# Unread products of old operands on TensorE inside its waits, in a two-layer hybrid trunk

## The reference, cut to what matters

```python
h = rmsnorm(x, norm1_g) * (1 + sc1) + sh1          # first norm
... = project_in(h, w_in)                          # then four token mixers
gate = sigmoid(h @ w_gate + b_gate)
merged = einsum('blnd,blnd->bld', gate, proj)      # proj: mixers @ w_branch
x = x + g1 * (merged @ w_out)
h2 = rmsnorm(x, norm2_g) * (1 + sc2) + sh2         # second norm
x = x + g2 * hier_moe(h2, ...)                     # 16 experts, top-1 group, top-2 expert
```

## Time and profile before

| | us |
|---|---|
| median of 3 runs | 2670.8 |
| lowest and highest | 2663.51, 2673.95 |
| the profiled execution's own time | 2673.33 |
| its span, first to last instruction | 2671.5 |
| mean granted TensorE clock in it | 0.942 |

### The profile page before, as it was taken

One profiled execution on the slowest core, in us unless ns is written; L12 is line 12 of the kernel. 1 busy time (PEld: TensorE's weight loads), 2 busy tenths in 40 slices (PEclk: granted clock), 3 DMA queues, 4 the chain that ended last, 5 costly groups with the idle time before them and its releaser, 6 DMA issues. The chain is left out here.

```text
span 2671.5 us, 33821 instructions
## 1 busy us (share of the span) xinstructions
PE 2484.2 (93%) x11748; PEld 1961.7 (73%) x11749; DVE 2061.3 (77%) x2682; ACT 1275.4 (48%) x1774; POOL 8.2 (0%) x16
## 2 busy tenths in 40 slices
PE   5699978999999998999998998799999999899997
PEld 2388745888888874878776886588888887777876
DVE  1499434888888874699898984488888888579988
ACT  2244243344343431688776443443434343277876
POOL 0000000000000000000000000000000000000000
PEclk8899887999999997899998998799999999799998
DMA  8988755776767658499886876277676675279986
GB/s 357 371 307 287 283 210 220 270 255 226 258 222 261 238 197 315 163 344 364 326 315 230 294 241 254 108 292 254 234 247 241 236 252 189 98 258 338 372 297 232
DMA packets 116660, 698.36 MB, mean 261 GB/s; under 512 B 24876, under 2 KB 30924, under 8 KB 33712
## 3 DMA queue, kind: packets, MB, share of 16 engines
q1 hardware_dynamic: 116528, 696.54, 71.4%
HBM read 691.97 MB, written 4.52 MB: 261 GB/s over the span
## 5 line engine op out<-in xcount | busy, mean ns | idle before, releaser
L607 ACT ACTIVATE high_w<-raw_w 128x1024 fp32r<-128x1024 f32 x904 | 942.9, 1054 | 794.2 <-PE bank L1633 684.1
L980 DVE TENSOR_TENSOR low_w<-raw_w,high_w 128x1024 fp32r<-128x1024 f32 x904 | 1076.7, 1211 | 180.4 <-ACT high_w L607 174.1
L1631 PE MATMUL bank<-high_w,in_high 128*128 128x512 f32 (+1 forms) x1600 | 625.0, 391 | 16.3 <-DVE low_w L980 16.3
L1632 PE MATMUL bank<-low_w,in_high 128*128 128x512 f32 (+1 forms) x1600 | 620.5, 388 | 0.0
L1633 PE MATMUL bank<-high_w,in_low 128*128 128x512 f32 (+1 forms) x1600 | 620.5, 388 | 0.0
L1631 PEld LDWEIGHTS bank<-high_w,in_high 128*128 128x128 f32 x1600 | 303.2, 190 | 89.3 <-issue 29.5
L1000 DVE SCALAR_TENSOR_TENSOR gate_mod_acc<-gate_mod_w,cond,gate_mod_acc 128x512 f32<-128x512 f32 x480 | 339.5, 749 | 23.3 <-issue 2.3
L1633 PEld LDWEIGHTS bank<-high_w,in_low 128*128 128x128 f32 x1600 | 302.9, 189 | 60.8
L1632 PEld LDWEIGHTS bank<-low_w,in_high 128*128 128x128 f32 x1600 | 303.2, 190 | 59.6
L2027 PE MATMUL bank<-high_w,win_high 128*128 128x512 f32 x512 | 206.2, 403 | 12.0 <-issue 6.7
L2028 PE MATMUL bank<-low_w,win_high 128*128 128x512 f32 x512 | 202.2, 395 | 0.0
(11 more groups left out here) (236 smaller groups left out, 2630.5 us busy)
## 6 DMA issues: line engine op xcount, KB each, us to landing
raw_w<-in_w_gate SPq DMA_DIRECT2D x128, 1024.0 KB, 5.0
raw_w<-in_w_exp_gate_up SPq DMA_DIRECT2D x128, 1024.0 KB, 5.5
mod_w<-in_w_mod SPq DMA_DIRECT2D x96, 1024.0 KB, 7.9
raw_w<-in_w_in SPq DMA_DIRECT2D x64, 1024.0 KB, 5.7
gate_mod_w<-in_w_mod SPq DMA_DIRECT2D x64, 1024.0 KB, 7.1
raw_w<-in_w_exp_down SPq DMA_DIRECT2D x64, 1024.0 KB, 5.3
in_mod_w<-in_w_mod SPq DMA_DIRECT2D x32, 1024.0 KB, 7.1
raw_w<-in_w_branch SPq DMA_DIRECT2D x32, 1024.0 KB, 5.0
```

Source lines behind the costliest of these rows:

```text
L607: act.activation(high_w[:, part, ks, 0:width], raw_w[:, slot, ks, 0:width], ACT.Copy).then_inc(high_ready, 1)
L980: dve.tensor_tensor(low_w[:, part, ks, 0:width], raw_w[:, slot, ks, 0:width], high_w[:, part, ks, 0:width].bitcast(F32), ALU.subtract).the ...
L1631: pe.matmul(out, highs[:, kk, t, :], high_w[:, part, k, 0:width], start=start, stop=False)
L1632: pe.matmul(out, highs[:, kk, t, :], low_w[:, part, k, 0:width], start=False, stop=False)
```

## The change

A helper keep_clock makes a number of 128x512 products of an operand with itself (its first 128 columns stand still, its 512 columns move) into one bank. Nothing reads the results, and the next use of the bank starts afresh. It is called in four places of TensorE's program:

- at the start of layer 1, in front of its first norm: 20 products of hid_low, after a new wait until three of layer 0's four additions are done;
- in front of the wait for the last merged values, in both layers: 12 products of in_high;
- in front of the second norm, in both layers: 24 products of in_high;
- in front of the last return, in both layers: 9 products of hid_high, into the bank of the chunk pair that has been read.

The operands are those of products that are over.

```diff
--- before.py
+++ after.py
@@ -1681,6 +1681,11 @@
             def turn(bank, col, src, width=P):
                 return pe.transpose(bank[:, col:col + width], src, ident[0:src.shape[0], 0:src.shape[0]])
 
+            def keep_clock(bank, operand, products):
+
+                for _ in range(products):
+                    pe.matmul(bank[:, :], operand[:, 0:P], operand, start=True, stop=True)
+
             def route_logits(i):
 
                 t, g = i // KB, i % KB
@@ -1736,6 +1741,8 @@
 
             for l in range(DEPTH):
                 if l:
+                    pe.wait_ge(added, NCH * l - 1)
+                    keep_clock(turn_banks[0], hid_low[:, 0:2, :, :].rearrange("p k t n -> p (k t n)"), 20)
                     turn_quarter(l, 0)
 
                 def before_unit(j):
@@ -1914,12 +1921,14 @@
                         if b == 3:
                             dense_sums(mod_bank, gate_mod_acc, (1,), used)
                 at.rounds(pe, NCH, gates, {n: k for n, k in W_OUT_SLOTS.items() if n[:2] != "in"} | {"chunk": NCH, "merged": TILES})
+                keep_clock(turn_banks[0], in_high[:, 0:2, :, :].rearrange("p k t n -> p (k t n)"), 12)
                 pe.wait_ge(chunk_read, at.done("chunk"))
                 turn_merged()
                 w_out()
                 pe.wait_ge(dense_stored, STORES * (l + 1))
 
                 pe.wait_ge(router_in, 32 * (l + 1))
+                keep_clock(turn_banks[0], in_high[:, 0:2, :, :].rearrange("p k t n -> p (k t n)"), 24)
                 norm2(len(mod_stage(l, "norm")) * UPC // (2 * KB))
                 mod_step(0)
 
@@ -2098,6 +2107,7 @@
                             if g or h or not at.first:
                                 back(back_banks[h if g else (h + 1) % 2], (g - 1) % GROUP_N, at.done("chunk") - 1)
                 at.rounds(pe, NCH // 2, down_pair)
+                keep_clock(banks[2 * (at.done("chunk") % 2)], hid_high[:, 0:2, :, :].rearrange("p k t n -> p (k t n)"), 9)
                 back(back_banks[1], GROUP_N - 1, at.done("chunk"))
 
         @block.gpsimd
```

## The result

The changed kernel took 2653.04 us in the median of 6 runs (2647.81 to 2659.5), the kernel before 2668.18 us on the same chip (6 runs, 2660.01 to 2673.95). The ratio is 0.9949, with a 95% interval of 0.9926 to 0.9973: faster, by 15 us. The forecast was 2663.5 us with a range of 2656 to 2671, so the time lies outside, on the fast side, and "faster by over 0.5%", which the median just is (0.51%) and the interval leaves open, had been given 0.13. Against the kernel before, 7.3 us less was forecast (2663.5 beside the 2670.8 of its first three runs), and 15.1 us less was measured (2653.04 beside the 2668.18 of six). Three more comparisons of the two kernels came later: ratios 0.9937 [0.9918, 0.9955], 0.9956 [0.9941, 0.9972] and 0.9936 [0.9917, 0.9955].

What follows compares the result with a forecast made beforehand. TensorE, busy 93% of the span, was taken as the bound, with half clock behind waits. Gains 3.3 + 3.2 + 1.8 + 0.5 + 0.5 = 9.3 us took 2673.33 to 2664.0; median put at 2663.5, range 2656 to 2671.

Steps and rivals of the forecast that it cites:

- The step that failed: TensorE's whole program: fetching the 220 added instructions was costed at nothing, beside weight transfers that run anyway.
- Merge: Last merged values and w_out: products and transposes at full instead of half clock, gaining 3.3 us in layer 0, 3.2 in layer 1.
- Rival 1: The clock falls after the block at the merge; each merge keeps 0.5 us, time 2668.5 us; chance 0.22.
- Last returns: Last return in each layer: four products at full clock and an earlier end, 0.9 us each, 1.8 together.
- the first norm: Layer 1's start: the first four transposes run at full clock, 0.45 us faster, counted as a gain of 0.5 us.
- Second norm, layer 1: First transposes start fast, gaining 0.5 us; the clock was expected to fall early in the loop.
- Second norm, layer 0: About 2 us saved by fast transposes and first modulation products becomes a longer wait for mod_w transfer: gain 0.
- rival 2: Layer 0's second norm stays at full clock, 4 us less there and 1 in layer 1's: 2658.5 us; chance 0.16.
- the sign that the forecast of 0 had named: Layer 0's second norm: mod_w waits would grow by what the faster transposes save.
- Price of a product: Each unread 128x512 product in the four kinds of wait takes 0.227 us; all 110 hidden by the waits, costed at nothing.
- rival 3: The unread products run slowly, 0.427 us each, and the blocks overrun their waits by 14.8 us: 2688 us; chance 0.03.
- A rule weighed against a row: Merge: the skill's rule that transposes don't count as busy would give 2668.5 us; a trace row disagreed, so 2664.0 was kept.

## Why the prediction was right or wrong

**The step that failed** is "The instructions themselves are 220 beside the page's 23,497 of TensorE and its loads; I cost fetching them at nothing, beside weight transfers that run anyway." It asked what 220 more instructions cost to fetch, and no stage shows a cost of that kind. It did not ask what they move. Every instruction behind them lies elsewhere in the program, and two branches of the experts that had waited for a block of instructions, until TensorE had nothing left to run, no longer do: -3.5 and -4.6 us in the table, more than any other term. The row was there to see: an "issue" wait of TensorE at L2027, twice, 6.7 us in all, in the same view as the earlier trace rows. I read that view only at the sites of the change:

```profile
PE bank L2027 <- issue: 6.7, 2, 3.5
```

With a bound of -8 us on that term the range would have held the time; by the row alone, neither its sign nor its chance could be known.

**Merge** (3.3 and 3.2 us forecast): -2.6 and -3.1. Right in the mechanism, a little high, since in three of eight cases (four profiles, two layers) the clock still falls for 3.4 us just ahead of w_out. Rival 1 has its mechanism there, but it would have kept only 0.5 us of each. Its price was added up wrongly: 2664.0 with 5.5 us less gained is 2669.5, not 2668.5, and the 2668.5 of the paragraph on the rule and the range's upper end took the error over; the measured time lies at the other end.

**Last returns** (0.9 each): with the first norm, whose 0.5 came out as 0.46 (8.16 to 7.71), layer 0's return gave 0.88 (8.04 to 7.16) in every profile of the two kernels. The timeline after, beside the earlier trace rows:

```profile
1389.91 2.20 PE L1687 MATMUL bank<-hid_high 128*128 128x512 f32 x9
1392.74 0.49 PE L2089 MATMUL bank<-sorted_high,unsort 128*128 128x512 f32 x1 [0.63 <-DVE sorted_low L1556]
1393.07 0.39 PE L2090 MATMUL bank<-sorted_low,unsort 128*128 128x512 f32 x1
```

Layer 1's gave 0.4 in the mean, since the kernel before pays there only when the clock happens to fall in that wait: in its second profile it did not, so the 0.9 rested on the luck of the one profile.

```profile
2651.20 0.49 PE L2080 MATMUL bank<-sorted_high,unsort 128*128 128x512 f32 x1 [2.66 <-DVE sorted_low L1556]
```

**Second norm, layer 1** (0.5): 0.2, nothing that could be told from the scatter. The reason was right: the clock falls a few microseconds into the loop and stays there, which these windows over the stage show, the changed kernel above the one that holds it from inside:

```profile
2293.62:2324.92 31.30, 27.91 (x139) 26.06 (x139) 20.60 (x90) 6.83 (x14) 0.00 (x0) 0.56 0.00 1
```

```profile
2295.98:2321.12 25.14, 22.73 (x155) 20.18 (x155) 19.72 (x87) 6.54 (x14) 0.00 (x0) 0.86 0.01 2
```

**Second norm, layer 0** (0, with rival 2 at -4 us): -4.8 us between the first two profiles looked like rival 2, but the kernel before took 52.7 us in its second profile with no edit, and the kernel with this block alone 56.7. The means differ by 2.1 us with ranges that meet, and over all kernels the stage takes 50.9 to 56.7 us in the ten profiles with the full block and 52.7 to 56.5 in the seven with no full product in it; what of it belongs to the block stays open. The waits for mod_w there grew from 2.4 and 2.5 us to 3.1 to 4.9, the sign that the forecast of 0 had named.

**Price of a product** (0.227 us, hidden): right; the nine above step by 0.226 us (2.20 without the last one's 0.39, over 8 steps), and no wait ended late, so rival 3 fell. **A rule weighed against a row**: across the 3.3 us with eight transposes between the block and w_out, the clock held in three of four profiles of the changed kernel in layer 1 and in two of four in layer 0. By the rule of the Trainium skill ("TensorE: Matmul & The Clock Gate", Part 4), under which transposes do not count as busy, it would by the reading of the prediction have fallen in all eight; it fell in three, so the runs show both outcomes.

**The sum.** The terms that were forecast, 9.3 us, came out at 2.6 + 3.1 + 1.3 + 0.4 + 0.2 = 7.6, without layer 0's second norm. The rest is the experts with their branches, -8.1, layer 0's second norm, -2.1, and layer 1's mixers, which gave 4.2 back. So a forecast whose mechanisms mostly held missed the time by a term that has nothing to do with them, and the ratio of 0.995 must not be read as what the clock is worth: products of 2 columns alone gave 0.9962.

## What to carry to other kernels

Adding or removing instructions moves all that stands behind them; in a program with branches, read the rows that wait for "issue", and the longest duration of each branch line, before any change, and compare them again before its gain is credited. Where a stage that the change does not touch differs by as much as the ones it does, run the edit with its work taken out and its instructions left in. A block of unread products ahead of a wait pays if dense work follows at once (5.7 us over two merges here); ahead of layer 1's norm, a loop of transposes and small products, it gave 0.2 us, within the scatter, and two products inside that loop took the stage from 31 to 25 us in four of five profiles, though the times of the kernels overlap.

## What the runs showed of the hardware that was not expected

- A compare-and-branch of TensorE's sequencer takes 64 to 126 ns as a rule, and 3.7 to 4.3 us when its place in the program is bad, with 2.8 to 3.5 us of TensorE idle and 3.4 us at half clock behind it. 24 instructions ahead of it were enough to end that in layer 0; in layer 1 a kernel with 230 ahead has it and one with 202 has not. Here it comes once in a layer at most, and in the last 90 us of the stage no instruction packet arrives in 39 of the 40 stages. The Trainium skill, "Advanced Engine Details and Errata", section "Sequencer and Instruction Queues" (Control Flow Timing), gives about 108 ns for such a branch; the median here, 126, agrees, the longest do not.
- Short products are not free to pad with: 46 of the identity at the start of the program took 19.8 us of TensorE and cost some 9 us, 31 more in layer 1 took 11.1 us and cost 12.
- Whether the clock falls differs from one execution of a kernel to the next, and a stage that the change does not touch then moves by 6 us in one kernel (119.3 or 125.2 us in layer 1's mixers) and by 9.5 over all 20 profiles (layer 0's mixers). One profile of each kernel is not enough to credit a stage with such a difference.
